# mLSTM and short-convolution decoder layer: who loads the first weights of heads 2 and 3, and where two steps of the first block stand

## The reference, cut to what matters

```python
xn = rmsnorm(x, norm_gain)
proj = einsum('btd,dp->btp', xn, w_in)          # 1024 x (9*512 + 8)
gb, gc, hc, zc, q, k, v, o, zm, ig, fg = split(proj)
yc, conv_new = short_conv(gc * hc, conv_buf, conv_w)    # 3 taps, states read and written
y_conv = gb * yc * silu(zc)
...                                              # mLSTM over chunks of 128 tokens
s   = (q k^T) * d ;  num = s v + inter * (q c_prev) ;  den = sum(s) + inter * (q n_prev)
h   = num / max(|den|, exp(-m))
y_m = (rmsnorm(h) * gain * sigmoid(o)) * silu(zm)
out = concat(y_conv, y_m) @ w_out ;  y = rmsnorm(x + out, final_gain)
```

## Time and profile before

| | us |
|---|---|
| median of 3 runs (1112.3 to 1112.65) | 1112.46 |
| the profiled execution | 1110.13 |
| its span in the trace | 1108.3 |
| PE busy in it | 1062.8 (96%) |
| DVE, ACT, POOL busy | 540.1, 340.1, 256.0 |
| granted TensorE clock, mean | 0.995 |

### The profile page before, as it was taken

How to read it: one execution, slowest core, us unless ns; L and a number is a source line. 1 busy time by engine, 2 the same in 40 slices (tenths; PEclk the granted TensorE clock), 3 DMA queues, 4 the chain that set the end, 5 groups by cost and what they waited for, 6 DMA issues and landing times. The chain is left out here.

```text
span 1108.3 us, 17992 instructions
## 1 busy us (share of the span) xinstructions
PE 1062.8 (96%) x7186; PEld 602.2 (54%) x7186; DVE 540.1 (49%) x1005; ACT 340.1 (31%) x672; POOL 256.0 (23%) x333
## 2 busy tenths in 40 slices
PE   3899999999999999999999999999999999999995
PEld 3555546565666555546665555566655555444442
DVE  5786664557553434575534344755332323433333
ACT  6546434242412232434122323341122131111111
POOL 5002303021212223212122232111211121542422
PEclk9999999999999999999999999999999999999998
DMA  9474532033200211442003114410212062265651
GB/s 248 141 159 85 135 81 49 24 105 101 89 20 19 90 49 57 119 120 89 20 18 91 49 57 138 119 32 20 94 38 90 25 218 92 102 216 209 237 200 77
DMA packets 124184, 108.74 MB, mean 98 GB/s; under 512 B 42384, under 2 KB 109092, under 8 KB 124100
## 3 DMA queue, kind: packets, MB, share of 16 engines
q1 hardware_dynamic: 81952, 65.68, 20.7%
q0 software_dynamic: 7600, 25.03, 6.2%
q10 hardware_dynamic: 34548, 16.87, 5.7%
HBM read 65.43 MB, written 33.41 MB: 89 GB/s over the span
## 5 line engine op out<-in xcount | busy, mean ns | idle before, releaser
L799 PE MATMUL bank<-xTh,Wh 128*128 128x512 f16 (+2 forms) x1304 | 421.5, 342 | 8.1 <-DVE Wl L163 4.9
L800 PE MATMUL bank<-xTl,Wh 128*128 128x512 f16 (+2 forms) x1304 | 424.4, 342 | 0.0
L801 PE MATMUL bank<-xTh,Wl 128*128 128x512 f16 (+2 forms) x1304 | 424.0, 342 | 0.0
L801 PEld LDWEIGHTS bank<-xTh,Wl 128*128 128x128 f16 x1304 | 129.2, 99 | 120.5 <-issue 0.7
L799 PEld LDWEIGHTS bank<-xTh,Wh 128*128 128x128 f16 x1304 | 129.1, 99 | 116.4 <-DVE Wl L163 5.1
L800 PEld LDWEIGHTS bank<-xTl,Wh 128*128 128x128 f16 x1304 | 129.2, 99 | 108.9 <-issue 2.6
L808 PE MATMUL bank<-Wh,xTh 128*128 128x128 f16 x544 | 92.8, 219 | 0.6 <-DVE ysum L163 0.6
L809 PE MATMUL bank<-Wl,xTh 128*128 128x128 f16 x544 | 92.8, 219 | 0.0
L810 PE MATMUL bank<-Wh,xTl 128*128 128x128 f16 x544 | 92.8, 219 | 0.0
L163 ACT ACTIVATE tz<-bank 128x512 f32<-128x512 f32 x32 | 19.1, 597 | 145.1 <-PE bank L801 144.4
L671 POOL TENSOR_TENSOR ysumst<-ysum,ysumst 128x1024 f16<-128x1024 f32 x16 | 34.1, 2128 | 103.6 <-ACT ysumst L163 103.6
(11 more groups left out here) (336 smaller groups left out, 1518.7 us busy)
## 6 DMA issues: line engine op xcount, KB each, us to landing
wst<-in_w_in ACTq DMA_DIRECT2D x29, 512.0 KB, 3.8
xs<-in_x_prompt SPq DMA_DIRECT2D x22, 512.0 KB, 4.2
y_ops<-ysumst POOLq DMA_DIRECT2D x16, 512.0 KB, 3.2
w_ops<-xs SPq DMA_DIRECT2D x16, 448.0 KB, 3.8
out<-xs POOLq DMA_DIRECT2D x11, 512.0 KB, 2.9
Wh<-y_ops SPq DMA_DIRECT2D x12, 448.0 KB, 3.6
Wl<-y_ops SPq DMA_DIRECT2D x12, 448.0 KB, 4.3
y_ops<-yst POOLq DMA_DIRECT2D x16, 256.0 KB, 3.3
```

What stands on the lines that cost most here:

```text
L799: mm(out, wh[:, k, :], xh, start=(k == 0), stop=False)
L800: mm(out, wh[:, k, :], xl, start=False, stop=False)
L801: last = mm(out, wl[:, k, :], xh, start=False, stop=(k == KT - 1))
```

## The change

Three edits.

1. For heads 2 and 3 the loads of tiles 0, 1 and 2 leave ACT. SP issues each right behind the store of the slab that last used the same staging buffer: behind slabs 1, 2, 3 the tiles 1, 2, 0 of head 2, behind slabs 5, 6, 7 the tiles 2, 0, 1 of head 3. ACT's wait for `wo_low` goes with them. Head 1 keeps its loads on ACT, and the load of the states stays there for all heads.
2. PE turns the state rows ahead of K's third piece instead of halfway through V, so they use `T1` before the gate product of the first 512 tokens. DVE copies them out behind the first `gate_scan`, ahead of `split_w(0, 1)`.
3. `split_w(0, 3)` leaves tile V on ACT and DVE. It now stands in tile Q, on ACT behind the first gate columns, on DVE behind `select` and `kw`, directly ahead of `split_w(0, 4)`.

```diff
-SPLIT_AT_HALF = {Q: (4,), GC: (5,), HC: (6,), GB: (7,), ZC: (8,)}
+SPLIT_AT_HALF = {Q: (3, 4), GC: (5,), HC: (6,), GB: (7,), ZC: (8,)}
...
                 for slab in range(first_slab + 1, first_slab + 4):
                     store_slab(slab)
+                    load_w(sp, 2 + first_slab // 4, slab % STAGES)
...
                 if t == V and first and b == 0:
-                    pe.wait_ge(states_in, 16 * 2)
-                    use_t1(3)
-                    nc.tensor.transpose(T1[:, 0:STATES_IN], prow[0:STATES_IN, :], ident[0:STATES_IN, 0:STATES_IN]).then_inc(t1_full, 1)
                     columns(1, MIX, t1(g, b, "mix cols", first))
...
                     elif first and b == 0 and t == K:
                         for c in range(CH):
+                            if c == CH // 2:
+                                pe.wait_ge(states_in, 16 * 2)
+                                use_t1(2)
+                                nc.tensor.transpose(T1[:, 0:STATES_IN], prow[0:STATES_IN, :], ident[0:STATES_IN, 0:STATES_IN]).then_inc(t1_full, 1)
                             if c == CH - 1:
-                                gates(x_units(0), MIX, BT, 2)
+                                gates(x_units(0), MIX, BT, 3)
...
-            def x_end(b, t, first):
-                if first and b == 0 and t == V:
-                    split_w(0, STAGES)
...
                     act.wait_ge(w_low, (g + 1) * NT)
-                    act.wait_ge(wo_low, 4 * g)
-                    for t in range(STAGES):
-                        load_w(act, g + 1, t)
+                    for t in range(STAGES) if g == 0 else ():
+                        load_w(act, 1, t)
                     act.wait_ge(cs_out, (g + 1) * 16)
                     load_states(act, g + 1)
...
-            gate_logits(1, BT, 2)
+            gate_logits(1, BT, 3)
...
                     for tile in SPLIT_AT_HALF.get(t, ()):
-                        if tile < NT - 1:
+                        if STAGES < tile < NT - 1:
                             gain_w(0, tile + 1)
                         split_w(0, tile)
...
                             gain_w(0, STAGES)
                             gain_w(0, STAGES + 1)
-                            split_w(0, STAGES)
...
-            GATE_COUNTS = [1, 2] + [t1(0, b, "gates", True) for b in range(NB - 1)]
+            GATE_COUNTS = [1, 3] + [t1(0, b, "gates", True) for b in range(NB - 1)]
...
             gate_scan(0, 0, MIX)
+            dve.wait_ge(t1_full, 3)
+            mark(copy(par[:, 0:STATES_IN], T1[:, 0:STATES_IN]).then_inc(t1_free, 1), t1_free, 3)
             split_w(0, 1)
             gate_abs(1, BT)
             gate_turn(0, 0, MIX)
             split_w(0, 2)
-            dve.wait_ge(t1_full, 4)
-            mark(copy(par[:, 0:STATES_IN], T1[:, 0:STATES_IN]).then_inc(t1_free, 1), t1_free, 4)
             gate_scan(1, MIX, BT)
```

More of the change, by code:

```diff
@@ L1302, in act_block @@
                     at_half(g, b, t, first)
-                    if t in (HC, GB):
-                        x_end(b, t, first)
                     evacuate(g, b, t)
-                    if t not in (HC, GB):
-                        x_end(b, t, first)
                     at_end(g, b, t, first)
```

## The result

| | before | after |
|---|---|---|
| median (4 runs each, in turn on one chip) | 1112.38 us | 1105.31 us |
| lowest, highest | 1110.55, 1112.65 | 1104.24, 1105.72 |
| the profiled execution | 1110.13 | 1105.21 |
| its span | 1108.3 | 1103.2 |

The ratio is 0.9938 (95%: 0.9926 to 0.9949): 6.9 us faster, between 5.7 and 8.2. Three of before's four runs are the ones that the forecast started from. The forecast was 1107.2 with a range down to 1105.8, so the time lies 0.5 us under the range. Against the profiled execution the sum said 1104.89, and the profiled execution of after took 1105.21.

A forecast was written before the change was run, and what follows sets the result against it. The prediction took PE as the bound, busy 1062.8 of 1108.3 us, so only its idle time could be won. 3.19 + 1.30 + 0.75 = 5.24 us off 1112.46 gave 1107.2 us, range 1105.8 to 1110.2.

The forecast's parts named there:

- K's copies: Heads 1 and 2, last blocks: PE's two waits for ACT's copy of K go whole, 1.27 + 1.92 = 3.19 us.
- The state updates: One later wait of 0.65 us for DVE's state update in each of two blocks goes: 1.30 us, bounds 0 and 1.30.
- The DVE idle row in front of `gain_w`: Sign of being wrong: DVE idle in front of `gain_w` near 59 or 458 us.
- the state updates stay late: Rival, chance 0.20: tile 0's load lands at 459 or later, the two 0.65 us remain; gain 3.94, time 1108.5.
- ACT is still held: Rival, chance 0.10: the states' load issues slowly for its own reason, K is copied late; gain about 2.0, time 1110.4.
- The first block: State rows and fourth split together: DVE's gate chain starts earlier, and 0.75 us reaches the block's end; bounds 0 and 2.2.
- the new waits for the chain: First block, Q's gate columns: PE arrives near 43.9 us and waits about 0.9 us for DVE's gate chain, ending at 44.7.
- GC's wait: First block: PE reaches GC's products at 53.3 us, waits 0.4 us for the later split, starts at 53.75 instead of 55.41.
- tile 6 in time: First block: load issued at 53.8 us lands at 58.2, used at 59.3, cover 1.1; the rival of slower had 0.03.
- the first operation of `gate_scan(1)` starts 0.75 to 0.8 us earlier: DVE, first block: with the state-row copy out of the gate chain, it starts at 38.3 us instead of 39.09.
- The median of the runs is 2.33 us above that execution; the difference is taken over unchanged: Last step of the sum: from 1104.89 us for the profiled execution to a median of 1112.46 - 5.24 = 1107.2.
- the first block gives nothing: Rival, chance 0.13: PE's idle time before `sel` brings a slower clock that eats the 0.75; gain 4.49, time 1108.0.

The follow-up runs named there:

- e6_act_behind_k: Kernel before, but ACT issues the three weight loads and the states' load of heads 2 and 3 behind its copy of K: 1111.42 us, ratio 0.9995.
- e23_block: Kernel before with only the state rows turned ahead of K's third piece and the fourth split moved to tile Q: 1111.67 us, ratio 0.9995.
- e5_pad: Changed kernel plus 18 one-column memsets on DVE behind `split_w(0, 1)`: 1105.18 us, ratio 0.9941 to before.
- POOL's gains: Changed kernel with `gain_w` of tiles 3 and 4 of head 0 moved from DVE to POOL: 1105.31 us, ratio 0.9936 to before.
- e3_split: Kernel before with only the fourth split moved behind Q's first columns, state rows left in V: 1111.59 us, ratio 1.0004.
- a1_look: Changed kernel without any edit, a single profiled execution: 1105.42 us.

## Why the forecast was right, and where it failed

**K's copies (3.19 us): right, a little more in size.** Both waits are gone. From the profiled execution of before to that of after it is worth 1.44 us in head 1's last block (the idle 1.27 and 0.17 more behind it) and 2.09 in head 2's, 3.53 in sum.

**The state updates (1.30): right in place, about half in size.** DVE starts `gain_w` at 457.49 (forecast 457.8). The wait of 0.65 at the earlier trace rows is gone and gives 0.76, but 0.29 us are lost again two steps on, and 0.1 after that. In the next head 0.91 are won and 0.55 lost, most of it at this row:

```profile
712.02 0.49 PE L863 MATMUL bank<-v,dp 128*128 128x129 f32 x2 [0.29 <-DVE cn L163]
```

That leaves 0.36 in each head, 0.72 in sum. The DVE idle row in front of `gain_w`, which the forecast named as a sign of being wrong, did come (1.09 us, for the load). Edit 1 measures 4.3 to 4.9 us by the two landmarks, against the several traces without it, where the sum said 4.49: two terms that miss by 0.3 and 0.6 us in opposite directions, so its closeness is in part luck. The rival "the state updates stay late" fell, since head 2's first load landed at 457.5 and not at 459. "ACT is still held" fell: the states' issue took 0.37 us. Its 3.01 us before go with the three loads in front of it (in e6_act_behind_k it takes 3.04 again behind three loads).

**The first block (0.75): the mechanism right, the term twice too large.** 0.35 us were measured. What the forecast said is in the rows: V's wait gone, the new waits for the chain (1.40, forecast 0.9) and `sel` (2.48 in e23_block, 0.79 after, where PE came later because its clock was low; forecast 2.4), GC's wait 0.47 (forecast 0.4), tile 6 in time, `dpm` at 75.35 (forecast 75.0). The step that was mis-sized is "the first operation of `gate_scan(1)` starts 0.75 to 0.8 us earlier": it counted the 0.51 us pause in front of the copy as part of the copy's cost. Only the 0.26 us copy and about 0.1 of its surroundings left the chain; the pause stayed with the 44th instruction. e5_pad, by moving it, took 0.40 more off the block (and lost it again behind the block).

**A term that the sum did not have.** From the start of PE's last matmul to the end of the span it is 11.96 to 12.00 us in all nine traces without edit 1, and 11.54 to 11.56 in all nine with it: 0.43 us. The engines' rows behind that matmul stand at the same distances up to SP's last issue. What differs is how long the last two stores of the output take to land, and the end waits for them. The rows are of before and of after (KB each, median us to landing); the last store alone takes 2.41 to 2.44 us in the first nine traces and 1.99 or 2.00 in the other nine.

```profile
out<-xs SPq DMA_DIRECT2D x2, 256.0 KB, 2.4
...
out<-xs SPq DMA_DIRECT2D x2, 256.0 KB, 2.0
```

Why they land sooner with edit 1 no experiment asked, and it stays open.

**The median: the step that failed.** The parts in sum are 4.3 to 4.9 in the heads, 0.35 in the first block and 0.43 at the end: 5.1 to 5.7 us, against a forecast of 5.24. By the profiled execution (1110.13 to 1105.21) the forecast held to 0.3 us. What failed is the last step of the sum, "The median of the runs is 2.33 us above that execution; the difference is taken over unchanged", and the range, which has terms for the waits and none for how executions scatter. Measured, before's median lies 2.25 us above its profiled execution (1112.38 against 1110.13) and after's 0.10 us above its own (1105.31 against 1105.21). Over all executions on record before's median is 1.5 us above (1111.60). The profiled execution was of before's lower group, the three runs that gave the median were all of the upper one, and the four of after all of its lower one. I took a difference between two draws for a constant of the kernel. With the 1.6 to 1.9 us between the groups in the range, its low end would have been near 1104, and the time in it.

Does the change itself move executions to the lower group? Of before 36 in 82 lie in the upper one; of the kernels with edit 1 in them (after, edit 1 alone, the padded one, POOL's gains) 7 in 35. One possible reason is in the traces: the `kf` wait of 1.9 to 2.2 us near 681, with a fall of the clock in two of the eight traces in which that wait stands. Edit 1 removes it, which at 1.2 to 1.4 us each is 0.3 to 0.4 us on average. Whether that is the whole of it is open: the other places (28 to 36, 54 to 62) are shared by both kernels, and 82 and 35 executions don't settle their shares.

**The rival "the first block gives nothing"** was half right: the clock does fall behind 51.6 (e23_block, e3_split, a1_look). It is hidden in the wait for `dpm`, all of it in a1_look and all but 0.2 us in e23_block, as its price said for a fall that comes once.

## What to carry to other kernels

When one late event holds two chains, mend it where both hang on it: taking K's copy out from behind the loads alone won nothing (0.9995), taking loads and copy off the wait won 5.5 us (ratio 0.9953). A wait on PE disappears only as far as the engine behind it comes sooner, so trace that engine's own chain to the end of the block, and do not count a pause beside a moved instruction as part of that instruction. A shorter stretch is not yet a shorter kernel: the padding took 0.40 us off the first block, and PE waited them out again behind it. And look at how the executions of one kernel lie before carrying an offset from a profiled one to a median of three: with two groups some 1.7 us apart, that distance belongs in the range.

## What the runs showed of the hardware

- DVE pauses 0.46 to 0.52 us at fixed places of its instruction stream (before its 44th, 281st and 579th instruction in the traces without padding), whatever the instruction is; 18 instructions put in front moved the pauses to other work. An 8 KB transfer of the kind "instruction" starts within 3 us behind each; that it is the cause is not shown.
- The time to issue the states' load on ACT's queue was 0.37 us with no weight loads issued just ahead of it, and 3.01 to 3.64 us right behind three weight loads.
- A DVE operation on 4x64 elements with two inputs in SBUF took 1.89 us beside a POOL operation of 1.90 us, and 0.22 without it.
- PE's clock fell below its upper level between 36 and 60 us in all 18 traces, a second time at 28 to 36 or 54 to 62 in some, in 2 of the 8 traces with a wait of 1.9 to 2.2 us near 681, and with one of 2.04 us at 489 but not with one of 2.40 at 713 (e6_act_behind_k). A further stretch costs 1.2 to 1.7 us where PE sets the pace, and nothing where DVE does.
- The last store of the output took 2.41 to 2.44 us to land in the nine traces without edit 1, and 1.99 or 2.00 in the nine with it.
